# Two transformer blocks on one core: how a projection's weight pieces are dealt over the last attention of block two

## The chip, the core and the metric

The kernel runs on one core of one Trainium2 chip. The metric is the device time of one execution in microseconds (us); lower is better. TensorE does the matrix products, VectorE and ScalarE the elementwise work, GpSimd (POOL) small work and stores, and SyncE (SP) issues the loads. Each engine works through its own program in order and waits on semaphores.

## The reference

The function computes two blocks, one after the other. The second is a two-layer block over 256 latent rows `x` and 256 context rows `ctx`, of width 2048. The part that matters here is its last layer:

```python
u = h @ o_w_in                              # 256 + 256 rows, 4416 columns
y1 = mixer_c(u[:, :1536], ...)              # 8 heads of 128, RMS norm of q and k, rotary, 2 kv heads
y2 = mixer_d(u[:, 1536:2368], ...)          # latent attention: q from w_q_b, k and v from w_kv_b, 8 heads
y  = concatenate([y1, y2]) * silu(u[:, 2368:])
x  = x + gate * (y @ w_o)                   # gate comes from silu(c) @ w_mod + b_mod
out = rmsnorm(x, final_g)
```

All arrays are fp32. Queries are the 256 latent rows, keys the 512 context and latent rows.

## The kernel before

**Weights.** A weight matrix comes in pieces of 128 x 1024 fp32 (512 KB). SP loads piece n into one of 8 buffers `raw` (`sp_chunk`, L371 to L376), once piece n-8 has been split. ScalarE rounds it to fp32r (`w_hi`, `split_hi`, L388), once TensorE has used up piece n-4 (there are 4 buffers), and VectorE subtracts to get the rest (`w_lo`, `split_lo`, L394). TensorE then does three matmuls for each 128 x 512 tile and row tile: hi by hi (L413), lo by hi (L417), hi by lo (L418); for the modulation vector (`mod`) only two (L413, L415). They are called weight matmuls below. A finished group of columns is evacuated from its accumulator bank by ScalarE (L467), with the function Silu for the gate columns, and stored by POOL (L556). The next group of columns in the same bank waits for that evacuation.

**The last attention** is the region `at3`. It has six passes: two of mixer C (C0 and C1, 8 softmax units each, a unit being 128 queries of one head against 512 keys) and four of mixer D (D0 to D3, 4 units each). The region takes along the weight stage `rest3`, whose 66 pieces are dealt over the passes: `qb` (3 groups of 2 pieces), `kvb` (4 of 1), `g` (3 of 8, Silu), `mod` (4 of 8). In matmuls a `g` piece is 12, a `mod` piece 4, a `qb` piece 12, a `kvb` piece 24; the stage has 584 in all. Piece numbers run from 0 (`qb`) over 10 (`g0`), 18 (`g1`), 26 (`g2`) to 34 (`mod0`), 42, 50 and 58 (`mod3`).

Each pass has the same order on TensorE (`Region.pe`): "row places" with weight matmuls alone; then a wait until VectorE has shaped the pass's rows (norm, rotary; the DVE lines 1719 to 1725 and 1597 to 1602); the transpositions of q and k (L1086); the place "units" with weight matmuls; then the unit loop, with iteration u doing the scores of unit u (L1102), the transposition of unit u-2's probabilities (L1117), the value product of unit u-3 (L1129) and the weight matmuls of place u. In the loop VectorE takes the row maximum (L1226) and later scales the output (L1210, L1218), and ScalarE does exp (L1159), then the splits of its place, then the copy of unit u-2's transposed probabilities (L1168), for which the next unit's transposition waits, there being one bank for them.

VectorE's order ahead of a pass is:

```python
                for p in self.passes:
                    for x in p.row_places:
                        self.lo(dve, p, x)
                    if p.shape_ops:
                        dve.wait_ge(rows_in, 16 * p.rows_end)
                        p.shape_ops(dve, link, p)
```

ScalarE does in each place, row places too, first the evacuation of the groups that ended in the place before, then its splits.

`shares` says how the matmuls are dealt. One tuple a pass: (number of row places, share of each, share of "units", share of the unit loop, spread over its places). The share is a place's part of the 584 matmuls. A split is put one or two places ahead of the piece's first matmul (`hi_at`, `lo_at`). SP loads a pass's value rows (L1049) ahead of piece first + 6, where first is the piece that the pass's first row place begins; that load waits until the pass before has done its last value product, since it overwrites the buffer, and the pieces behind it in SP's queue wait with it.

The matmuls by place, worked out from the shares:

| | C0 | C1 | D0 | D1 | D2 | D3 |
|---|---|---|---|---|---|---|
| row places | 144 | 12 | 24 | 15 | 8 | 16 |
| units | 24 | 21 | 9 | 18 | 20 | 0 |
| loop | 84 | 84 | 39 | 38 | 28 | 0 |
| splits (lo) in row places | - | 2 | 1 | 4 | 4 | 0 |

Of the kernel before, what the change touches and what calls it, by code (L numbers as in the profile page):

```python
# [115 lines left out]
def two_blocks(nc, A, C, out):  # L116
    ctx = ExitStack()
    with ctx:
# [1624 lines left out]
        def passD(it):  # L1743
# [20 lines left out]
            for g in range(2):  # L1764
                for qt in range(2):
# [4 lines left out]
            return p  # L1770

        at3 = Region([passC(it) for it in range(2)] + [passD(it) for it in range(4)], stages["rest3"],
                     [(7, 24, 12, 88), (1, 24, 12, 88), (1, 24, 12, 40), (1, 24, 12, 40), (1, 20, 10, 30), (1, 16, 0, 0)],
                     (6, 7), (6,), (7,), pb3, pt3, lambda pe: None)


# [411 lines left out]
```

How the kernel before makes its waits and increments, by code:

```python
        def wait_done(eng, s, bank):  # L364
            if bank in s.done:
                eng.wait_ge(acc_done[bank], s.done[bank] + 1)
            else:
                eng.wait_ge(w_used, s.no[len(s.chunks) - 1] + 1)
# [1 line left out]
        def sp_chunk(sp, g, c):  # L371
            n = g.no[c]
            if n >= RAWS:
                sp.wait_ge(lo_ready, n - RAWS + 1)
            dst = raw[:, n % RAWS, 0:g.wtiles * g.width].rearrange("p (k n) -> p k n", k=g.wtiles)
            sp.dma_start(dst, g.chunks[c]).then_inc(landed[n % RAWS], 16)
# [6 lines left out]
        def split_hi(act, s, c):  # L383
            n, size = s.no[c], s.wtiles * s.width
            act.wait_ge(landed[n % RAWS], 16 * (n // RAWS + 1))
            if n >= SPLITS:
                act.wait_ge(w_used, n - SPLITS + 1)
            nc.scalar.activation(w_hi[:, n % SPLITS, 0:size], raw[:, n % RAWS, 0:size], ACT.Copy)\
              .then_inc(hi_ready, 1)
# [1 line left out]
        def split_lo(dve, s, c):  # L391
            n, size = s.no[c], s.wtiles * s.width
            dve.wait_ge(hi_ready, n + 1)
            nc.vector.tensor_tensor(w_lo[:, n % SPLITS, 0:size], raw[:, n % RAWS, 0:size],
                                    w_hi[:, n % SPLITS, 0:size].bitcast(F32), ALU.subtract)\
              .then_inc(lo_ready, 1)
# [1 line left out]
        def pe_chunk(pe, s, c, first=0, upto=None):  # L398
# [2 lines left out]
            upto = pairs if upto is None else upto  # L401
            if first == 0:
                pe.wait_ge(lo_ready, n + 1)
            for i in range(first, upto):
```

## Time and profile before

| | |
|---|---|
| device time, median of 3 runs | 3595.54 us (3592.03 to 3596.17) |
| profiled execution | 3594.34 us |
| its span, first to last instruction | 3592.5 us |
| TensorE busy | 3281.4 us, 91% of the span |
| VectorE busy | 1731.5 us, 48% |
| ScalarE busy | 1484.9 us, 41% |
| mean granted TensorE clock | 0.957 of full |
| region `at3` from its first transpositions to its last value product | 3178.18 to 3441.48 us |

"Idle before" is the time an engine stood still ahead of a group of instructions, and the name behind the arrow what ended it. Times of an instruction are from the span's start; a matmul's duration overlaps the next one's, so spacing tells more than duration.

### The profile page before, as it was taken

Reading aid. Unit: us, or ns where it says so; the run is one execution under the profiler, and the core shown is the slowest. Engines: PE = TensorE matmul, PEld = TensorE weight load, DVE = VectorE, ACT = ScalarE, POOL = GpSimd, SP = SyncE. Lnnn points to the kernel's source line nnn. Section 1 sums busy time; section 2 is a strip of 40 time slices with the busy share of each in tenths; the row PEclk is TensorE's granted clock in tenths of the full one; section 3 lists DMA queues with packets and bytes.
Section 4 is the critical chain, followed back from the end, with each engine's and each line's share of the span. In section 5 each row is a group of like instructions: output and inputs, shape, how many; then the busy total and the mean of one; then the engine's idle time right before and its main releaser. Section 6 shows DMA issues by size and latency. Waiting matters only on the chain.

```text
span 3592.5 us, 39327 instructions
## 1 busy us (share of the span) xinstructions
PE 3281.4 (91%) x15207; PEld 2640.4 (73%) x15207; DVE 1731.5 (48%) x2446; ACT 1484.9 (41%) x2198; POOL 223.4 (6%) x340
## 2 busy tenths in 40 slices
PE   6999999999999999999959999999966979788857
PEld 5888888778888787887848777778755868665546
DVE  3446555566566656556542233334433343344534
ACT  3444444434554545546552223333422143244522
POOL 0000000000000000000010000000021000110010
PEclk9999999999999999999969999999987979898978
DMA  6867745566777767778723322324242324544653
GB/s 186 281 206 232 247 130 165 166 220 211 229 242 261 257 229 252 252 246 269 233 86 123 125 71 95 107 99 132 96 138 107 98 75 152 175 146 140 207 182 123
DMA packets 355269, 628.10 MB, mean 175 GB/s; under 512 B 44619, under 2 KB 111848, under 8 KB 352268
## 3 DMA queue, kind: packets, MB, share of 16 engines
q1 hardware_dynamic: 320572, 543.49, 46.7%
q0 software_dynamic: 18528, 62.93, 4.9%
q10 hardware_dynamic: 15984, 19.17, 1.6%
q8 instruction: 121, 1.98, 0.2%
q14 instruction: 64, 0.52, 0.0%
HBM read 579.86 MB, written 51.94 MB: 176 GB/s over the span
## 4 chain that ended last, share of the span: by engine, by line
PE 82%; DVE 6%; ACT 4%; issue 3%; DMA 2%; POOL 1%; ACTq 1%; SPq 0%; DVEq 0%; POOLq 0%
PE acc L413 25%; PE acc L418 22%; PE acc L417 22%; PE acc L1102 3%; PE acc L1129 3%; DVE w_lo L394 2%; PE acc L415 2%; PE acc L1117 2%; ACT w_hi L388 1%; PE acc L1086 1%; PE acc L648 1%; PE acc L1106 1%; ACTq L1261 1%; ACT aff L682 1%; PE acc L738 0%
## 5 line engine op out<-in xcount | busy, mean ns | idle before, releaser
L394 DVE TENSOR_TENSOR w_lo<-raw,w_hi 128x1024 fp32r<-128x1024 f32 (+1 forms) x986 | 1161.1, 1210 | 836.8 <-ACT w_hi L388 819.1
L413 PE MATMUL acc<-w_hi,a_hi 128*128 128x512 f32 (+4 forms) x3800 | 1507.9, 397 | 59.0 <-DVE w_lo L394 24.0
L417 PE MATMUL acc<-w_lo,a_hi 128*128 128x512 f32 (+4 forms) x3800 | 1472.0, 387 | 0.0
L418 PE MATMUL acc<-w_hi,a_lo 128*128 128x512 f32 (+4 forms) x3800 | 1471.8, 387 | 0.0
L388 ACT ACTIVATE w_hi<-raw 128x1024 fp32r<-128x1024 f32 (+1 forms) x986 | 1001.4, 1046 | 817.7 <-PE acc L418 793.9
L413 PEld LDWEIGHTS acc<-w_hi,a_hi 128*128 128x128 f32 x3800 | 718.9, 189 | 226.2 <-DVE w_lo L394 50.5
L418 PEld LDWEIGHTS acc<-w_hi,a_lo 128*128 128x128 f32 x3800 | 718.2, 189 | 146.5
L417 PEld LDWEIGHTS acc<-w_lo,a_hi 128*128 128x128 f32 x3800 | 719.3, 189 | 130.8 <-issue 0.7
L1226 DVE TENSOR_REDUCE at_st<-acc 128x1 f32<-128x256 f32 (+3 forms) x208 | 101.3, 487 | 445.3 <-PE acc L1102 300.7
L1159 ACT ACTIVATE pb<-acc,at_st 128x256 f32<-128x256 f32 (+3 forms) x208 | 108.8, 523 | 379.1 <-DVE at_st L1226 355.8
L648 PE MATMUL acc<-ident,xn 128*128 128x128 f32 x224 | 57.8, 426 | 124.6 <-DVE xn L1827 49.0
L413 PE MATMUL acc<-w_hi,MV 128*128 128x512 f32 x384 | 156.1, 406 | 5.4 <-DVE w_lo L394 4.2
L415 PE MATMUL acc<-w_lo,MV 128*128 128x512 f32 x384 | 151.3, 394 | 0.0
L648 PEld LDWEIGHTS acc<-ident,xn 128*128 128x128 f32 x224 | 41.2, 219 | 140.9 <-DVE xn L1827 50.4
L556 POOL DMA_DIRECT2D U<-stage x98 | 53.5, 548 | 963.2 <-ACT stage L467 962.7
L1117 PEld LDWEIGHTS acc<-ident,pb 128*128 128x128 f32 (+1 forms) x528 | 63.5, 142 | 65.7 <-issue 56.3
L1168 ACT ACTIVATE pt<-acc 128x256 f32<-128x256 f32 (+3 forms) x208 | 89.7, 431 | 53.0 <-PE acc L1117 53.0
L467 ACT ACTIVATE stage<-acc 128x512 f32<-128x512 f32 (+2 forms) x100 | 55.9, 595 | 130.7 <-PE acc L418 118.2
L1117 PE MATMUL acc<-ident,pb 128*128 128x128 f32 (+1 forms) x528 | 95.9, 281 | 10.5 <-ACT pt L1168 10.4
L413 PEld LDWEIGHTS acc<-w_hi,MV 128*128 128x128 f32 x384 | 72.4, 188 | 30.5 <-DVE w_lo L394 11.4
L415 PEld LDWEIGHTS acc<-w_lo,MV 128*128 128x128 f32 x384 | 72.6, 189 | 14.7
L1210 DVE RECIPROCAL at_st<-at_st 128x1 f32<-128x1 f32 x208 | 33.9, 163 | 80.6 <-PE acc L1129 75.9
(326 smaller groups left out, 1732.3 us busy)
## 6 DMA issues: line engine op xcount, KB each, us to landing
raw<-in_w_mod SPq DMA_DIRECT2D x192, 512.0 KB, 5.4
raw<-in_w_mlp_in SPq DMA_DIRECT2D x128, 512.0 KB, 4.6
raw<-in_w_mlp_out SPq DMA_DIRECT2D x128, 512.0 KB, 5.3
raw<-in_e_w_in SPq DMA_DIRECT2D x104, 512.0 KB, 5.0
raw<-in_w_in SPq DMA_DIRECT2D x96, 512.0 KB, 4.6
raw<-in_w_in SPq DMA_DIRECT2D x88, 472.0 KB, 4.7
raw<-in_w_o SPq DMA_DIRECT2D x64, 512.0 KB, 4.8
raw<-in_o_w_in SPq DMA_DIRECT2D x64, 512.0 KB, 4.5
```

What stands on the lines that cost most here:

```text
L388: nc.scalar.activation(w_hi[:, n % SPLITS, 0:size], raw[:, n % RAWS, 0:size], ACT.Copy)\
L394: nc.vector.tensor_tensor(w_lo[:, n % SPLITS, 0:size], raw[:, n % RAWS, 0:size], w_hi[:, n % SPLITS, 0:size].bitcast(F32), ALU.subtract)\
L413: nc.tensor.matmul(o, s.lhs(0, kt, tt), wh, start=kt == 0, stop=False)
L415: last = nc.tensor.matmul(o, s.lhs(0, kt, tt), wl, start=False, stop=end)
L417: nc.tensor.matmul(o, s.lhs(0, kt, tt), wl, start=False, stop=False)
L418: last = nc.tensor.matmul(o, s.lhs(1, kt, tt), wh, start=False, stop=end)
L648: last = nc.tensor.transpose(acc[:, self.bank(u), j * P:(j + 1) * P], self.src(i)[:, (b * 4 + j) * P:(b * 4 + j + 1) * P], ident[:, :])
L1102: last = nc.tensor.matmul(acc[:, bank, 0:w.keys], w.q[x], w.k[x], start=x == 0, stop=x == n - 1 and w.bias is None)
L1117: last = nc.tensor.transpose(acc[0:kk, bank, x * P:(x + 1) * P], self.pb[:, v % self.npb, x * P:x * P + kk], ident[:, :])
L1129: last = nc.tensor.matmul(acc[:, self.obanks[v % len(self.obanks)], 0:P], self.pt[0:kk, v % 2, x, :], vt, start=x == 0, stop=x == len(w.v) ...
L1159: nc.scalar.activation(self.pb[:, v % self.npb, 0:w.keys], acc[:, 4 + v % 2, 0:w.keys], ACT.Exp, bias=st[:, 0:1], accum_out=st[:, 1:2]).th ...
L1226: ins = nc.vector.tensor_reduce(m, acc[:, 4 + v % 2, 0:w.keys], AX.X, ALU.max, negate=True)
```

## The change

The shares of `at3` alone. What each pass deals to its row places grows (from C1 on), what it deals to the unit loop is halved or less, and C1 to D3 get 4, 2, 2, 2 and 2 row places in place of one each.

```diff
         at3 = Region([passC(it) for it in range(2)] + [passD(it) for it in range(4)], stages["rest3"],
-                     [(7, 24, 12, 88), (1, 24, 12, 88), (1, 24, 12, 40), (1, 24, 12, 40), (1, 20, 10, 30), (1, 16, 0, 0)],
+                     [(7, 24, 12, 44), (4, 27, 12, 44), (2, 22, 10, 16), (2, 22, 10, 16), (2, 18, 8, 8), (2, 14, 0, 0)],
                      (6, 7), (6,), (7,), pb3, pt3, lambda pe: None)
```

The instructions stay the same ones; only their order on each engine changes. The matmuls by place are then:

| | C0 | C1 | D0 | D1 | D2 | D3 |
|---|---|---|---|---|---|---|
| row places | 144 | 102 | 42 | 41 | 34 | 26 |
| units | 24 | 12 | 12 | 6 | 8 | 0 |
| loop | 48 | 42 | 15 | 20 | 8 | 0 |
| splits (lo) in row places | - | 8 | 3 | 8 | 8 | 3 |

C1's row places run from `g0` piece 4 to the middle of `g1` piece 4, and its last split there is `g1` piece 5. Group `g0` ends in C1's second row place, as before in a row place; `g1` ends in C1's loop place 6 (before in place 8), `g2` in D1's first row place in both. C1's loop places 0 to 9 have 6, 3, 3, 6, 3, 6, 3, 3, 6 and 3 matmuls (before 9, but 6 in places 4 and 8), C0's have 9, 3, 6, 3, 6, 3, 3, 6, 3 and 6 (before 9, but 6 in places 4 and 8). The first pieces behind SP's load of value rows are `g1` piece 2 (C1), `g2` piece 7 (D0), `mod0` piece 5 (D1) and `mod2` piece 3 (D2).

## Rows read from the trace of the kernel before

**Rows 1.** Waits over 3170 to 3441.5: us in total, times, longest us.

```profile
PE acc L1086 <- DVEq L1181: 40.6, 5, 16.8
```

**Rows 2.** Busy time by stretch: us, then PE, PEld, DVE, ACT, POOL busy (instructions), PEclk, DMA share, GB/s.

```profile
3187.94:3228.14 40.20, 37.80 (x197) 28.68 (x196) 16.79 (x29) 22.08 (x38) 2.17 (x4) 1.00 0.39 136
3228.14:3247.96 19.82, 3.00 (x15) 2.16 (x13) 16.10 (x23) 0.51 (x1) 3.23 (x3) 0.70 0.38 119
3247.96:3259.85 11.89, 9.20 (x33) 7.39 (x34) 1.82 (x2) 5.79 (x7) 1.17 (x2) 0.64 0.64 188
3259.85:3296.72 36.87, 36.87 (x197) 28.90 (x196) 17.92 (x30) 20.21 (x35) 1.08 (x2) 1.00 0.31 98
...
3296.72:3307.45 10.73, 10.31 (x56) 8.28 (x55) 6.12 (x18) 3.04 (x5) 0.73 (x1) 1.00 0.78 252
...
3307.45:3330.03 22.58, 22.58 (x104) 14.75 (x103) 8.74 (x14) 11.02 (x18) 0.00 (x0) 1.00 0.38 117
3330.03:3339.60 9.57, 3.66 (x19) 2.72 (x17) 8.15 (x18) 2.12 (x2) 0.73 (x1) 0.94 0.79 257
3339.60:3350.16 10.56, 9.51 (x38) 7.34 (x39) 3.22 (x4) 6.98 (x10) 1.10 (x2) 0.73 0.80 260
3350.16:3373.86 23.70, 22.67 (x103) 14.50 (x102) 15.26 (x21) 17.18 (x26) 0.53 (x1) 1.00 0.64 216
3373.86:3383.16 9.30, 2.11 (x11) 1.38 (x9) 8.78 (x19) 2.53 (x3) 0.73 (x1) 0.80 0.82 276
3383.16:3393.37 10.21, 8.90 (x40) 6.88 (x41) 3.74 (x5) 5.73 (x8) 0.52 (x1) 0.85 0.94 301
3393.37:3415.62 22.25, 20.39 (x94) 12.62 (x92) 14.08 (x19) 13.77 (x22) 0.52 (x1) 1.00 0.33 116
3415.62:3421.16 5.54, 3.90 (x19) 2.90 (x17) 5.02 (x16) 0.00 (x0) 0.75 (x1) 1.00 0.64 160
```

**Rows 3.** Timeline of VectorE ahead of C1's and D1's shaping: start, us, instruction.

```profile
3228.89 2.35 DVE L394 TENSOR_TENSOR w_lo<-raw,w_hi 128x1024 fp32r<-128x1024 f32 x2
3231.16 1.22 DVE L1719 TENSOR_TENSOR tmp<-qC 128x1024 f32<-128x1024 f32 x1
...
3334.88 1.22 DVE L394 TENSOR_TENSOR w_lo<-raw,w_hi 128x1024 fp32r<-128x1024 f32 x1 [0.61 <-ACT w_hi L388]
```

**Rows 4.** Timeline of TensorE: two weight matmuls three apart, C0's second transposition, two iterations of C1.

```profile
3150.40 0.39 PE L413 MATMUL acc<-w_hi,a_hi 128*128 128x512 f32 x1
...
3151.08 0.39 PE L413 MATMUL acc<-w_hi,a_hi 128*128 128x512 f32 x1
...
3201.38 0.63 PE L1117 MATMUL acc<-ident,pb 128*128 128x128 f32 x4 [0.66 <-ACT pt L1168]
...
3281.20 1.02 PE L1102 MATMUL acc<-kCT,qCT 128*128 128x512 f32 x2
3282.06 0.60 PE L1117 MATMUL acc<-ident,pb 128*128 128x128 f32 x4
...
3285.46 1.02 PE L1102 MATMUL acc<-kCT,qCT 128*128 128x512 f32 x2
```

**Rows 5.** Timeline of ScalarE: a copy, C1's evacuation of `g1`, a split in D1's row place.

```profile
3283.67 0.59 ACT L1168 ACTIVATE pt<-acc 128x512 f32<-128x512 f32 x1
...
3290.99 1.28 ACT L467 ACT_TABLE_LOAD   x1
3292.28 1.09 ACT L467 ACTIVATE stage<-acc 128x512 f32<-128x512 f32 x2
...
3333.78 1.06 ACT L388 ACTIVATE w_hi<-raw 128x1024 fp32r<-128x1024 f32 x1 [1.66 <-PE acc L418]
```

**Rows 6.** SP's queue at D1: value rows, then weight pieces.

```profile
3330.30 1.90 SPq L1049 DMA_DIRECT2D kvD<-KVB  x4
3332.25 4.47 SPq L376 DMA_DIRECT2D raw<-in_w_mod  x6
```

**Rows 7.** Time from issue to landing of weight pieces, 3325 to 3430.

```profile
DMA to landing us min/median/max: 3.8/6.4/11.2
```

## The prediction

> **What bounds the kernel now.** TensorE is busy 91% of the span, so I read only where it is not, in the region that the change touches. The chain of waits for that stretch names one large item: TensorE waits 40.6 us for the shaping of rows on VectorE, ahead of five of the six passes, 16.8 us of it ahead of C1 [rows 1]. Cut into stretches, each pass has three parts: from the first weight matmul behind the last value product (call it T0) to the transpositions, from there to the first scores, and the unit loop up to the next T0 [rows 2]. The reader should see TensorE nearly full in the loops (36.87 of 36.87 us in C1) and nearly empty ahead of the transpositions (3.00 of 19.82 in C1, 2.11 of 9.30 in D2). The 584 weight matmuls are the same before and after, so the change can only gain by putting them where TensorE is idle now, and it loses what stays idle elsewhere once they are gone. I work out the parts again, pass by pass.
>
> **Prices.** A weight matmul is (3151.08 - 3150.40)/3 = 0.227 us [rows 4], a `g` piece 2.7, a `mod` piece 0.9. A split is 1.06 on ScalarE [rows 5] and 1.2 on VectorE [rows 3]. An iteration of C1 with 9 weight matmuls takes 3285.46 - 3281.20 = 4.26, so 2.22 without them; the transposition begins 0.86 behind the scores; the copy that frees the next transposition ends 3283.67 + 0.59 - 3281.20 = 3.06 behind the scores, about 4.1 with a split ahead of it [rows 4, 5].
>
> **C1, the row places.** They go from 12 matmuls to 102, 23.1 us of work over a gap that was 16.8. If shaping began when it does now, the gap would be gone. But VectorE does all splits of the row places ahead of the shaping, and there are 8 now, not 2; the two before are in the trace right ahead of it [rows 3]. The last of them needs `g1` piece 1 used up on TensorE. From T0: the four `g0` pieces end at 10.9; ScalarE has one split to finish (to 12.0), loads the Silu table (1.28) and evacuates a bank (0.6, half of the 1.09) [rows 5], so `g1` starts at 13.8; two pieces later it is 19.3; split on ScalarE to 20.4, on VectorE to 21.6. Shaping took 3247.96 - 3231.16 = 16.8 [rows 2, 3], so the transpositions start at 38.4. TensorE's matmuls end at 26.1 and it idles some 12 us again, plus 2.9 before `g1`. The part goes from 19.82 to 38.4: +18.6 for 90 matmuls worth 20.4. The whole cover buys 1.8 us.
>
> **C1, to the first scores.** Before 11.89 [rows 2], with 21 matmuls, the wait for the evacuation of `g0` and the low clock (0.64 over this stretch). The evacuation now lies in the row places. Transpositions 2.9, 12 matmuls 2.7 and 0.7 for the low clock at their start: 6.3, so -5.6.
>
> **C1, the loop.** 42 matmuls less, -9.5, if nothing surfaces. Three things do. (a) At the start the second transposition waits for a copy 4.1 behind the third scores, a split being ahead of it; 9 matmuls filled that, 3 leave about 1.6. (b) `g1` ends in place 6 rather than 8, so its evacuation falls between two exps: Silu table 1.28, evacuation 1.09, Exp table 1.28, then exp and copy (0.69 and 0.59): the copy ends 3.06 + 4.9 = 8.0 behind the scores of unit 6, where TensorE wants to go on at 2.9 + 2.4 = 5.3; about 2.9 with the hand-overs. Before, it came behind the last exp and cost nothing. (c) Two splits ahead of the last copy, with 3 matmuls beside them: 0.7. So +5.2 - 9.5 = -4.3. C1 in all: +18.6 - 5.6 - 4.3 = +8.7.
>
> On (b) a rule weighs in: a switch of tables takes 1.28 us in the trace, and the next instruction starts 0.01 behind it [rows 5]. The Trainium skill (ScalarE: Activation LUTs, section "What ACT_TABLE_LOAD costs") adds a drain of about 1.38 us to each switch. By the row, (b) has two switches for 2.6 us, by the page 5.3, which would make the sum 2.8 us larger; the row decides.
>
> **C0's loop.** 36 matmuls less. The second transposition stands at 3201.38 whatever they do: it waits for ScalarE [rows 4], which is held by the stores of `kvb`. So the 9 matmuls taken from places 0 to 2 buy nothing; the 27 behind them buy 6.1, less 0.3 where a split meets 3 matmuls: -5.8.
>
> **D0.** Shaping is short (3.5 us) and three splits ahead of it take some 5 us from T0, so its 42 matmuls (9.5 us) still cover it. To the first scores it goes from 33 matmuls to 54: +4.7 on 10.73 [rows 2]. Loop: 24 less, -5.4, and 0.3 surfaces. Sum -0.4.
>
> **D1.** Before, ScalarE's last split of the row place ended 4.8 behind T0 and VectorE's 6.1 [rows 3, 5]. Now `g2`'s evacuation (2.4) and four more splits follow: VectorE's last ends at 13.0, shaping takes 3339.60 - 3336.10 = 3.5, the transpositions start at 16.6, against 9.57: +7.0. To the first scores: 12 matmuls less, and the evacuation no longer there: 10.56 to 6.2, -4.4. Loop: 18 less, -4.1, plus 0.8 for three splits ahead of the last copy. Sum -0.7.
>
> **D2.** Eight splits again, but `mod2` piece 3 and all behind it are issued only 3332.25 - 3330.03 = 2.2 behind T0, because SP's load of value rows waits for the last value product [rows 6]. Landing takes 3.8 to 6.4 us (least and median) [rows 7]. Before, all four split pieces were ahead of that point. ScalarE meets piece 3 before `mod1`'s evacuation, so `mod2` starts late: from the end of that split 0.6 + four pieces of 0.9 + 1.06 + 1.2 + hand-overs and shaping 4.2 = 10.7. With landing 3.8 the transpositions start at 17.8, with 6.4 at 20.4; the piece finds DMA almost free, so I take 18.5 against 9.30: +9.2. To the first scores 10.21 to 6.2 (12 matmuls and `mod1`'s evacuation less): -4.0. Loop: 20 less, -4.5, and 1.3 surfaces: -3.2. Sum +2.0.
>
> **D3.** Three splits come ahead of the shaping, none before. Row part 5.54 to 5.2 + 3.6 = 8.8: +3.3. The rest stays.
>
> **Sum.** -5.8 + 8.7 - 0.4 - 0.7 + 2.0 + 3.3 = +7.1 us. On the profiled execution 3594.34 + 7.1 = 3601.4; the median of the runs is 1.2 above that execution, so 3602.6. Ends of the unknown sizes: the stalls in the loops (2 to 14 us in place of about 10: each needs one wait to lie as I place it) and D2's landing (-0.7 to +1.9) give 3595 to 3609.
>
> **Rivals.** (1) The loops have slack. If none of the stalls in the loops surfaces (C0 2.4 with the fixed transposition, C1 5.2, D0 0.3, D1 0.8, D2 1.3: 10.0), the sum is -2.9, 3592.7. For it: C1's loop showed no idle time at all with a split in most places [rows 2]. Against it: that was with 9 matmuls an iteration, and C0 waited even so [rows 4]. (2) Not slower, but clearly faster: shaping isn't held back. If VectorE began it as early behind T0 as now, C1's transpositions would stand at TensorE's own 26.1 in place of 38.4, D1's at 12.3 for 16.6, D2's at 12.2 for 18.5, D3's at 5.9 for 8.8: -25.8, so -18.7 and 3576.8. It decides at whether the shaping of C1 starts before 10 us behind T0. The program order speaks against it. (3) The clock. TensorE's granted clock is 1.00 up to C1's idle stretch and 0.70 over it, 0.80 over D2's [rows 2], half speed (1.2 of 2.4 GHz) within. New idle stretches of 3 us before `g1` and nearly 5 before `mod2` may bring it down there, in front of matmuls on which the splits wait: 24 matmuls at twice the time in C1 (+5.4) and 16 in D2 (+3.6): 3611.6.
>
> **How the numbers follow.** A measurement here can tell about 0.2%, 7.2 us. My forecast has 0.56, rival 1 0.17, rival 2 0.06, rival 3 0.21. The forecast lies on the border: of its 0.56 some 0.31 is above +7.2 and 0.25 within. With rival 3 slower is 0.51; with rival 1 same is 0.41; faster is 0.08. The range runs from rival 1 to just past rival 3's.
>
> **What the profile would show.** Right: C1's shaping starts 21 to 22 us behind T0, with 8 w_lo splits ahead of it, and TensorE idles about 12 us there still; its matmuls before it stop near 11 us for the evacuation; a table load between two exps of C1's loop, with 2 to 3 us of wait at a transposition; D2's transpositions 18 us behind T0. Wrong: a gap ahead of C1's transpositions under 5 us (rival 2), a loop of C1 of about 27 us rather than 32.6 (rival 1), granted clock under 1.00 in the first 25 us of C1's row places (rival 3).

## The result, and the profile after

The changed kernel takes 3607.44 us (median of 7 runs, 3603.87 to 3615.84) against 3595.54 (7 runs, 3591.52 to 3597.22): a ratio of 1.0041, 95% interval 1.003 to 1.0053, so slower, by about 14.7 us. The medians differ by 11.9 us, the means (3609.45 and 3594.64) by 14.8, which is what the ratio gives. The profiled execution has a span of 3604.6 us, 12.1 more than the one of before. TensorE's mean granted clock is 0.955, against 0.957.

The stretches of the changed kernel, cut at the same events as [rows 2]: C0 from its transpositions to its first scores, C0's loop, then row part, start and loop of C1; D0's row part with its start, D0's loop; row part, start and loop of D1 and of D2; D3's row part. Columns as there.

```profile
3178.57:3190.05 11.48, 10.21 (x36) 8.16 (x37) 1.82 (x2) 3.75 (x7) 2.25 (x4) 0.66 0.61 171
3190.05:3222.48 32.43, 29.48 (x161) 22.02 (x160) 13.92 (x27) 19.13 (x35) 2.16 (x4) 1.00 0.28 102
3222.48:3263.28 40.80, 25.26 (x106) 20.13 (x104) 24.17 (x30) 9.53 (x10) 4.34 (x5) 0.85 0.46 161
3263.28:3269.84 6.56, 6.56 (x24) 5.56 (x25) 0.69 (x1) 3.42 (x4) 0.00 (x0) 0.61 0.33 82
3269.84:3302.76 32.92, 29.62 (x156) 22.36 (x154) 13.62 (x27) 19.71 (x34) 1.17 (x2) 0.95 0.26 82
3302.76:3318.28 15.52, 15.11 (x76) 12.27 (x76) 9.38 (x20) 2.91 (x5) 0.72 (x1) 1.00 0.77 259
3318.28:3335.80 17.52, 17.49 (x80) 10.08 (x79) 6.47 (x12) 9.05 (x16) 0.00 (x0) 1.00 0.26 75
3335.80:3352.35 16.55, 11.14 (x44) 7.87 (x43) 13.01 (x23) 10.63 (x12) 1.82 (x3) 0.83 0.89 307
3352.35:3358.37 6.02, 6.02 (x26) 4.90 (x27) 2.80 (x4) 1.79 (x3) 0.00 (x0) 0.60 0.44 162
3358.37:3378.63 20.26, 18.77 (x85) 11.06 (x84) 10.21 (x16) 13.66 (x21) 0.53 (x1) 1.00 0.58 184
3378.63:3399.30 20.67, 10.22 (x37) 7.47 (x35) 14.61 (x24) 7.66 (x8) 1.25 (x2) 0.81 0.89 318
3399.30:3406.14 6.84, 6.84 (x28) 5.53 (x29) 1.37 (x2) 1.78 (x3) 0.00 (x0) 0.59 0.12 35
3406.14:3424.53 18.39, 15.97 (x74) 8.96 (x72) 8.25 (x14) 10.36 (x18) 0.52 (x1) 1.00 0.35 106
3424.53:3433.71 9.18, 6.93 (x29) 4.54 (x27) 8.66 (x19) 2.96 (x3) 0.75 (x1) 1.00 0.76 235
```

The reader should compare the third row with C1's of [rows 2]: the row part grew from 19.82 to 40.80 us, TensorE's busy time in it from 3.00 to 25.26. The first three rows and D2's row part (the row of 20.67 us) carry the story; the loops shrank by 3 to 8 us each, as the matmuls left them.

VectorE's timeline ahead of C1's shaping, and the waits of TensorE in C1 (the Silu evacuation of `g0`, the transpositions, the copy in the loop) and in D2 (the evacuation of `mod1`):

```profile
3234.81 1.23 DVE L394 TENSOR_TENSOR w_lo<-raw,w_hi 128x1024 fp32r<-128x1024 f32 x1 [1.49 <-ACT w_hi L388]
3242.60 1.22 DVE L394 TENSOR_TENSOR w_lo<-raw,w_hi 128x1024 fp32r<-128x1024 f32 x1 [6.57 <-ACT w_hi L388]
3245.33 1.23 DVE L394 TENSOR_TENSOR w_lo<-raw,w_hi 128x1024 fp32r<-128x1024 f32 x1 [1.51 <-ACT w_hi L388]
3246.47 1.22 DVE L1719 TENSOR_TENSOR tmp<-qC 128x1024 f32<-128x1024 f32 x1
```

```profile
3236.83 0.47 PE L413 MATMUL acc<-w_hi,a_hi 128*128 128x512 f32 x1 [3.21 <-ACT stage L467]
...
3263.28 1.97 PE L1086 MATMUL acc<-ident,qC 128*128 128x128 f32 x8 [12.33 <-DVEq L1181]
...
3295.14 0.63 PE L1117 MATMUL acc<-ident,pb 128*128 128x128 f32 x4 [2.13 <-ACT pt L1168]
...
3387.37 0.77 PE L413 MATMUL acc<-w_hi,MV 128*128 128x512 f32 x1 [5.66 <-ACT stage L467]
```

The shaping starts at 3246.47, which is 24.0 us behind T0 (3222.48); before, it started 3.0 us behind T0 (3231.16 less 3228.14). VectorE stood idle 6.57 us before one of the splits that it must do first. TensorE then waits 12.33 us for the shaping, against 16.8 before [rows 1].

### The profile page after: what moved, and what is told of

Same layout as the page of the kernel before. It is cut to its first block, busy times and chain, and to the rows that moved or that the text cites. A ratio compares the mean times of both kernels' runs of the same rounds, so it can differ in the third digit from the quotient of the medians.

```text
span 3604.6 us, 39327 instructions
## 1 busy us (share of the span) xinstructions
PE 3293.1 (91%) x15207; PEld 2646.7 (73%) x15207; DVE 1732.4 (48%) x2446; ACT 1482.7 (41%) x2198; POOL 223.1 (6%) x340
## 4 chain that ended last, share of the span: by engine, by line
PE 82%; DVE 6%; ACT 4%; issue 3%; DMA 2%; POOL 1%; ACTq 1%; SPq 0%; DVEq 0%; POOLq 0%
PE acc L413 25%; PE acc L417 22%; PE acc L418 22%; PE acc L1102 3%; PE acc L1129 3%; DVE w_lo L394 2%; PE acc L415 2%; PE acc L1117 2%; ACT w_hi L388 2%; PE acc L1086 1%; PE acc L648 1%; PE acc L1106 1%; ACTq L1261 1%; ACT aff L682 1%; PE acc L738 0%
```

## The experiments

All compare the median and the ratio with runs of the kernel before on the same chip. "Under the changed kernel's median" means under 3607.44, which was measured with other runs of the kernel before (median 3595.54, in the experiments 3592.52 to 3594.52), so such a difference is uncertain by up to 3 us; the stretches of the traces are the finer measure. Edits are against the changed kernel unless said otherwise. A tuple's shares are parts of the sum over all tuples, so a kernel that changes some of them also moves a few matmuls in the passes whose tuple it leaves alone.

### The shares of the C passes alone

```diff
-  [(7, 24, 12, 44), (4, 27, 12, 44), (2, 22, 10, 16), (2, 22, 10, 16), (2, 18, 8, 8), (2, 14, 0, 0)]
+  [(7, 24, 12, 44), (4, 27, 12, 44), (1, 24, 12, 40), (1, 24, 12, 40), (1, 20, 10, 30), (1, 16, 0, 0)]
```

> The new shares for C0 and C1 alone, the old ones for D0 to D3. The changed kernel's own trace gives C1's row part +21.0 us and the other parts of C0 and C1 -17, +3.9 in all; here g1 ends one place later, behind the last exp, so the 3 us that its evacuation cost in C1's loop go too. Theory of the splits ahead of the shaping: C1's shaping still starts about 24 us behind the last value product and the kernel is 0 to 3 us slower than before. Rival (the loss sits in the D passes alone, C1's longer cover pays): 5 us or more faster than before.

3597.17 us against 3593.75, ratio 1.0012 (1.0003 to 1.0021): slower by 3 to 4 us, a little more than the 0 to 3 expected. In the profiled execution C0 and C1 together take 0.7 us more than before (119.2 against 118.5), and the D passes, whose tuples are the old ones, 3.0 us more. C1's row part is 41.5 us. Its loop, with the same 42 weight matmuls as in the changed kernel but `g1` ending behind the last exp:

```profile
3270.28:3298.36 28.08, 27.80 (x155) 20.79 (x154) 13.83 (x27) 18.07 (x33) 1.17 (x2) 1.00 0.31 96
```

28.08 in place of 32.92 us: the loop has 4.84 us of stalls that hang on where pieces and evacuations fall. Even without them, C0 and C1 gain nothing from the longer cover. The rival, 5 us faster than before, fell.

### The shares of the D passes alone

```diff
-  [(7, 24, 12, 44), (4, 27, 12, 44), (2, 22, 10, 16), ...
+  [(7, 24, 12, 88), (1, 24, 12, 88), (2, 22, 10, 16), ...
```

> The old shares for C0 and C1, the new ones for D0 to D3. The changed kernel's trace gives the D passes +6.5 us in all, 11.4 of gain and loss in D2's row part alone. If the parts add up, 5 to 9 us slower than before, with the transpositions of D2 about 20 us behind T0. Rival (the loss is C1's): within 3 us of before.

3604.76 against 3593.75, ratio 1.0028 (1.0017 to 1.0038): slower by about 10 us, at the upper end of the 5 to 9 that I expected or past it (the ratio's interval is 6 to 14). D2's transpositions stand 20.83 us behind T0, as in the changed kernel. In the profiled execution the D passes take 149.3 us from D0's T0 to D3's last value product, against 143.6 before: +5.7, as expected. C0 and C1 take 5.0 us more as well (123.5 against 118.5): although their tuples are the old ones, C1 now has 9 matmuls and three splits in its row place and 27 matmuls in "units", in place of 12, two and 21, and from its transpositions to its first scores it takes 14.62 us in place of 11.89, at a granted clock of 0.60 in place of 0.64. Another 3.1 us lie ahead of the region, where nothing differs. So this run does not put the whole 10 us on the D passes.

### Shaping among the splits

In outline (the helper functions are left out; the wait for the rows stays ahead of the shaping):

```diff
                     for x in p.row_places:
-                        self.lo(dve, p, x)
+                    splits(early[0])                    # C1: 3, D1: 4, D2: 3
                     if p.shape_ops:
                         ...
-                        p.shape_ops(dve, link, p)
+                        p.shape_ops(dve, woven, p)      # woven: link, then splits(early[step])
+                        splits(all that are left)
```

> The new shares, and VectorE does the shaping of C1, D1 and D2 among the row places' splits in place of behind them (C1: three splits first, the rest between the shaping's steps; D1 four first, D2 three first). Nothing else moves. Theory: C1's transpositions come 27 to 29 us behind T0 in place of 40.8, D1's about 2 and D2's about 3 us earlier, so 14 to 18 us less than the changed kernel: 3590 to 3594, not slower than before. Rival (the row places are long for another reason: the clock, the evacuation of g0, late weights): under 5 us less than the changed kernel.

3589.49 against 3593.75, ratio 0.9985 (0.9976 to 0.9994): faster than before, and 18 us under the changed kernel's median. The row parts of C1, D1 and D2:

```profile
3218.63:3250.69 32.06, 25.86 (x106) 19.96 (x104) 22.59 (x29) 9.51 (x10) 4.34 (x5) 0.95 0.61 205
3321.22:3336.13 14.91, 11.40 (x44) 8.79 (x43) 12.89 (x23) 9.02 (x11) 1.82 (x3) 0.89 0.88 297
3362.14:3377.01 14.87, 9.70 (x37) 7.32 (x36) 13.01 (x23) 7.55 (x8) 1.25 (x2) 0.89 0.90 311
```

They lose 8.7, 1.6 and 5.8 us against the changed kernel (D2 more than the 3 us expected). All three moved as VectorE's order says; nothing else was changed. In C1 the rest of the row part is as it was: TensorE waits 3.21 us for the evacuation of `g0`, as in the changed kernel, and the 5.17 us of matmuls behind it run at a mean clock of 0.67, as there. So neither that wait nor the clock behind it made the 8.7 us, which speaks against the rival. C1 stopped short of the 27 to 29 us that I expected, and the timelines of POOL and, last line, VectorE show why:

```profile
3233.12 1.10 POOL L556 DMA_DIRECT2D U<-stage  x2 [12.19 <-ACT stage L467]
3234.30 0.20 POOL L844 TENSOR_SCALAR rC<-rC 128x12 f32<-128x12 f32 x1
...
3236.91 1.23 DVE L1738 TENSOR_TENSOR qC<-qC,rC 128x1024 f32<-128x1024 f32 x1 [8.11 <-POOL rC L846]
```

The norm's power on POOL stands in its queue behind the store of `g0`, which waits for ScalarE's evacuation; VectorE waited 8.11 us for it in the middle of the shaping. I had not priced that queue, as in the changed kernel the store is long past when the shaping begins.

### The norm ahead of the store

The edit is against the woven kernel. Besides the lines shown, one of C1's splits moves to where VectorE waits for POOL:

```diff
-                        if x == "units" and p.norms:
+                        if x == first and p.norms:      # first: the pass's first row place
                             pool.wait_ge(at_ss, p.ss_end)
```

> The woven kernel (new shares, shaping of C1, D1 and D2 among the splits), and in C1 POOL does the power for the norm ahead of the store of g0, one more split standing in the wait for it. In the woven kernel's trace VectorE waited 8.1 us for that power, since POOL stood at the store until ScalarE's evacuation. Theory: the wait falls to about 2 us, C1's row part from 32.1 to 28 to 29 us, and 3 to 4 us come off the woven kernel. Rival (TensorE's own row places set those 32 us, at the low clock): no change of C1's row part beyond 1 us.

3585.89 against 3594.52, ratio 0.9982 (0.9973 to 0.9991). C1's row part falls from 32.06 to 28.16 us and VectorE's wait for POOL to 2.48:

```profile
3236.49 1.22 DVE L1741 TENSOR_TENSOR qC<-qC,rC 128x1024 f32<-128x1024 f32 x1 [2.48 <-POOL rC L846]
```

The medians differ by 3.6 us, but the runs of both kernels spread over 13 to 15 us, so the row part is the evidence, not the median.

### SP's value rows later

```diff
-  after.setdefault(min(n, p.first + RAWS - 2 if i else loads_at), []).append(("loads", p))
+  after.setdefault(min(n, p.first + RAWS - 2 + 6 if i else loads_at), []).append(("loads", p))
```

> The new shares, and SP's load of a pass's value rows stands six pieces later in its queue, so the weights of the row places no longer wait behind the last value product. Theory (D2's row part is 20.7 us and not 17.4 because mod2 piece 3 lands 7 us behind T0, and the evacuation of mod1 and the low clock follow from it): D2's transpositions 3 to 4 us earlier, the other passes unmoved, 3 us less than the changed kernel. Rival (the order of ScalarE's own work sets it): no change in D2.

3600.78 against 3593.75, ratio 1.0018 (1.001 to 1.0027), 6.7 us under the changed kernel's median. D2's row part:

```profile
3378.79:3394.12 15.33, 8.58 (x37) 6.04 (x36) 14.43 (x24) 7.34 (x8) 1.25 (x2) 0.91 0.97 332
```

15.33 in place of 20.67: 5.3 us, more than the 3 to 4 expected. TensorE's wait for the evacuation of `mod1` falls from 5.66 to 1.77 us, since ScalarE no longer stands at a piece that has not landed. The row parts of the other passes are within 0.2 us. In the changed kernel SP issued that piece at 3380.85 and ScalarE met it at 3385.69:

```profile
3385.69 1.06 ACT L388 ACTIVATE w_hi<-raw 128x1024 fp32r<-128x1024 f32 x1 [3.77 <-DMA raw<-in_w_mod]
```

### Plain copies for the gate columns

```diff
+        for g in in3[6:]:
+            g.evac["func"] = ACT.Copy
```

> The new shares, with the gate columns of g0, g1 and g2 evacuated by plain copies (the Silu on those 1536 columns is left out), so that ScalarE never leaves the exp table within the region. Everything else as in the changed kernel. If the two table loads around g1's evacuation set the wait in C1's loop, its 2.1 us wait goes and the low clock behind it too: the loop from 32.9 to 29 to 30.5 us; C1's row part loses 1.3 to 2 us, as the evacuation of g0 before g1 is shorter; 4 to 6 us less than the changed kernel in all. If it is the evacuation's place among the exps and not the tables, the loop loses under 1 us.

3600.52 against 3592.52, ratio 1.0021 (1.0011 to 1.003), 6.9 us under the changed kernel's median, where 4 to 6 were expected. C1's row part is 37.75 (3.0 less, where 1.3 to 2 were expected; the wait ahead of `g1` fell from 3.21 to 1.78 us), its loop:

```profile
3264.22:3293.43 29.21, 27.90 (x155) 20.88 (x153) 13.62 (x27) 17.02 (x32) 1.17 (x2) 1.00 0.31 96
```

3.7 us less, at a granted clock of 1.00 in place of 0.95, and the wait of 2.13 us is gone, with the evacuation still between two exps. So the two table loads, not the evacuation itself, made that stall. Not all of the kernel gained: D1's row part took 19.04 us in place of 16.55, as ScalarE stood for `mod` pieces that had not landed, once for 2.64 us. In the changed kernel they stand like this on ScalarE:

```profile
3290.04 1.28 ACT L467 ACT_TABLE_LOAD   x1
3291.33 1.08 ACT L467 ACTIVATE stage<-acc 128x512 f32<-128x512 f32 x2
3292.44 1.28 ACT L1159 ACT_TABLE_LOAD   x1
3293.73 0.69 ACT L1159 ACTIVATE pb<-acc,at_st 128x512 f32<-128x512 f32 x1
```

### C0's shaping woven too, with the new and the old shares

The first kernel joins all edits so far (but not the plain copies) and weaves C0's shaping among its splits, with the norm first on POOL there too. The second has the old shares and, of all edits, C0's weave with its norm first alone.

> As the last, with SP's value rows six pieces later and C0's shaping woven among its seven row places too. C0's transpositions waited 9.1 us for the shaping in every kernel so far, and VectorE had over 9 us of idle time while TensorE worked on the row places. Theory: that wait goes, 8 to 9 us less; with the late value rows another 0 to 2 in D2. 3576 to 3582. Rival (the wait moves to the stores of kvb, on which ScalarE stood at C0's start): 2 to 4 us less only.

> The old shares with C0's shaping alone woven. It tells what of the gain belongs to the new shares. Theory: 8 to 9 us less than before, 3585 to 3588. Rival as for the last kernel: 2 to 4 us less.

All woven: 3571.72 against 3594.52, ratio 0.9937 (0.9924 to 0.9949), 4 us below the 3576 to 3582 expected; why it gained that much more stays open, the median that it started from being that of a kernel whose runs spread over 15 us. Old shares: 3584.66 against 3594.52, ratio 0.9976 (0.9967 to 0.9985), just below the 3585 to 3588 expected. C0's wait of 9.07 us ahead of its transpositions, the same in each earlier kernel, is gone in both, and it stays gained (9.9 us between the medians of the old shares' kernel and the kernel before); the rival, that it moves to the stores of `kvb`, shows as 1.2 to 2.5 us at C0's start. The two kernels differ by some 13 us, but not in the shares alone: the first also has the shaping of C1, D1 and D2 woven, the norm first in C1 and the late value rows. C0 is woven in both, and there its loop is 5.1 us shorter with the new shares (35.38 against 40.51). How much of the rest belongs to the shares stays open, since the old shares with the other weaves were not run: they too have 2, 4 and 4 splits ahead of the shaping of C1, D1 and D2, and if all of them could go behind it, these row parts would be 3.0, 6.1 and 5.8 us shorter (an estimate: the row parts of [rows 2] less a shaping of 16.8, 3.5 and 3.5 us). What is shown is that the new shares, slower than before with VectorE's old order, are faster than before with the new one.

### Shares tuned to the woven order

Against the all-woven kernel, in place of its shares:

```diff
+  [(7, 24, 12, 44), (4, 26, 12, 50), (2, 24, 10, 16), (2, 20, 10, 20), (2, 16, 10, 16), (2, 10, 0, 0)]
```

> As the all-woven kernel with shares (7,24,12,44), (4,26,12,50), (2,24,10,16), (2,20,10,20), (2,16,10,16), (2,10,0,0): g1 ends in C1's place 7, so that its evacuation comes behind the last exp, and fewer splits lie ahead of the shaping in C1, D2 and D3. Theory: C1's loop loses its 2.1 us wait and part of the start's, 3 to 5 us less than the all-woven kernel. Rival (the evacuation's cost moves to the next wait of the loop): no change.

3568.51 against 3594.52, ratio 0.9927 (0.9914 to 0.9939): the fastest kernel of the study, some 26 us under before. C1's loop, with 48 weight matmuls:

```profile
3252.42:3281.90 29.48, 28.95 (x162) 22.22 (x160) 13.74 (x27) 18.73 (x34) 1.07 (x2) 1.00 0.49 152
```

The wait of 2.13 us is gone; the all-woven kernel's loop took 31.32 with 42. D2 still has eight splits in its row places; C1 has seven and D3 two. But the two kernels' intervals overlap, and the profiled execution of this one is the slower of the two (3572.4 to 3569.9 us), so whether it beats the all-woven one stays open.

## Why the prediction was right, and where it was short

The forecast, slower by 7.1 us at 3602.6, had the sign and the mechanism. The measured median, 3607.44, lies within its 3595 to 3609, near the upper end. (From the prediction's own terms the lower end is 3594: 3602.6 less 8 for the stalls and 0.7 for the landing.) The loss is 11.9 us by the medians and 14.7 by the ratio; the second, put on top of 3595.54, would be 3610.2, past that end. As a number the result stands between the forecast and rival 3's 3611.6, 4.8 above the one and 4.2 below the other, so the number alone does not choose between them; the steps do. In us, on the profiled execution:

| step | predicted | measured |
|---|---|---|
| C0, start and loop | -5.8 | -6.1 |
| C1, row places | +18.6 | +21.0 |
| C1, to the first scores | -5.6 | -5.3 |
| C1, loop | -4.3 | -4.0 |
| D0 | -0.4 | -0.3 |
| D1 (row +7.0, start -4.4, loop -3.3) | -0.7 | -1.0 |
| D2 (row +9.2, start -4.0, loop -3.2) | +2.0 | +4.1 |
| D3 | +3.3 | +3.6 |
| sum | +7.1 | +12.0 |

The steps hold nearly all of the 12.1 us by which the profiled spans differ. Of the 4.9 us that the forecast lacks, the row places of C1 and D2 are 4.6.

**VectorE's order.** Right, and shown by the weave. Ahead of C1 all eight splits came before the shaping, which started 24.0 us behind T0, not the 21.6 of the sum.

**The term that was mis-sized: C1's row places, by 2.4 us.** The sum priced the 54 matmuls behind the evacuation of `g0` at full clock. That was rival 3's point, and it happened in part: a granted clock under 1.00 in the first 25 us of C1's row places, which the prediction named as a sign of being wrong, is there. The granted clock around the wait, in the changed kernel (the wait, then the matmuls behind it):

```profile
3233.60:3236.83 3.23, 0.02 (x2) 0.03 (x1) 1.23 (x1) 3.08 (x4) 0.00 (x0) 1.00 1.06 400
3236.83:3242.00 5.17, 5.17 (x16) 4.10 (x17) 0.00 (x0) 0.83 (x2) 1.10 (x2) 0.67 1.04 391
```

The clock falls from 1.00 to 0.67 in the mean right behind an idle stretch of 3.2 us (eight matmuls from 3237.99 to 3240.97 stand 0.43 us apart in place of 0.227, which is the lower of the two levels); the two pieces that the last split waits for took 3244.24 - 3236.83 = 7.4 us up to that split on ScalarE, 5.4 in the sum, and `g1` had begun 0.5 us later than in the sum; the shaping came late with both. Rival 3 had +5.4 here; the clock came back within some microseconds, so it was under half.

**The other: D2's row places, by 2.2 us.** I took 18.5 between ends of 17.8 and 20.4; it was 20.67. The landing was 4.8 us, with which the sum gives 18.8; the other 1.9 us come with the low clock behind the 5.66 us wait for the evacuation, as in the next row, which starts where the matmuls go on:

```profile
3387.40:3394.50 7.10, 7.10 (x22) 5.33 (x22) 4.02 (x4) 4.11 (x4) 0.52 (x1) 0.73 1.05 394
```

The two mechanisms were priced apart, in the forecast and in a rival, though the one brings on the other. The late value rows gave 5.3 us back. But the weave alone gave 5.8 in D2 with the landing as it was (TensorE still waited 5.17 us for the evacuation of `mod1`), so the 20.67 us needed both the late piece and VectorE's order: either repair takes most of the loss away, and with both (the all-woven kernel) the part took 13.35 us.

**C0.** The second transposition stands at 3201.51, against 3201.38 [rows 4], with 9 matmuls less ahead of it and though the scores began 2.1 us later, so ScalarE sets it, as the step said. C0's start lost 1.7 us; in the kernel before it was:

```profile
3178.18:3187.94 9.76, 8.49 (x36) 6.90 (x37) 1.82 (x2) 4.10 (x7) 2.25 (x4) 0.83 0.54 144
```

That loss is not the change's: its work there is the same, and the part took 11.41 us in the kernel with the old shares for C0 and C1, 9.75 in the one with plain copies; its clock was 0.66 here, 0.83 before. The loop gives these 1.7 us back, since its second transposition stands where it stood.

**The loops.** C1's stalls came to 1.12 us at the second transposition and 2.13 at the table loads, with a low clock behind that; the sum had 1.6 and 2.9. The total fitted (5.2 us predicted, 5.5 measured, which is 32.92 less 36.87 - 9.5; the loop of the C-only kernel is 4.84 shorter), but in part by luck: the waits were 1.2 us shorter than in the sum, and the low clock behind the second, 0.76 in the mean over 7 us, which was not in the sum, cost about as much (an estimate: 1.7 us by that mean). On the table switch the row held [rows 5]: the exp starts 0.01 us behind the second load. The rule of the Trainium skill (ScalarE: Activation LUTs, section "What ACT_TABLE_LOAD costs"), a further drain of 1.38 us a switch, does not show in this trace. The plain copies took 3.7 us off the loop. That lies between the rows' 2.6 us for two switches and the 5.3 us that are an estimate by that figure of the Trainium skill, but the low clock is in it.

**The rivals.** Rival 1, loops with slack, fell: the stalls are in the trace, and C1's loop took 32.92 us, not about 27. Rival 2 decided at a shaping start before 10 us behind T0; it was 24.0. But it priced the right repair: woven, the row places gave back 8.7, 1.6 and 5.8 us. Rival 3 came in part, in C1 and in D2: its 9.0 us there were some 4.

What stays open: the ratio's 14.7 us are 2.6 above the profiled 12.1. The changed kernel's runs reach 3615.84, a spread of 12 us where before's is 6, and one execution can't tell which stretches make that up.

## What to carry to other kernels

Before filler work is dealt into the gap of a wait, ask what the filler itself queues ahead of the work that ends the wait. Here each weight piece that fills TensorE's gap needs a split on VectorE, the engine that TensorE is waiting for, and the splits stood first, so 20.4 us of cover bought a shaping that started 21 us later after T0. The same cover was worth it once the two were woven: 3589.49 us, 4 us less than before in place of 12 more; and then the next queue in order (POOL's store ahead of the norm) showed itself. And count what a stall leaves behind: the two table loads between two exps of C1's loop are 2.6 us, the wait that they made was 2.13, and without them the loop was 3.7 us shorter, the low clock behind the wait being gone too.

## What the runs showed of the hardware

Behind waits of 3.2 and 5.7 us TensorE ran 5 and 7 us at a mean clock of 0.67 and 0.73, which the sum had left out. And the same instructions can run at either level: in the woven kernel's profiled execution, D3's loop ran at a granted clock of 0.59 though TensorE was busy 24.28 of its 25.31 us; before, the same instructions took 16.32 us at 1.00. The waits ahead of it were short, 2.26 us before D3's transpositions and 0.68 before its first scores, and the kernel with the norm first had 2.24 and 0.68 there, with a loop of the old length. The two, woven kernel first, then before:

```profile
3414.43:3439.74 25.31, 24.28 (x64) 11.37 (x64) 4.31 (x10) 5.70 (x13) 0.51 (x1) 0.59 0.10 38
```

```profile
3425.16:3441.48 16.32, 14.67 (x64) 7.83 (x64) 4.31 (x10) 5.72 (x13) 0.51 (x1) 1.00 0.45 167
```

That is 9 us in one place, more than half of that kernel's spread of 3582.8 to 3595.7 us over its runs. No experiment was made on what brings it on.
